# Other orders of instructions around a recurrence's front, its inverse and a gate, and two squares on ScalarE

## The reference

```python
# first block
z = rms_norm(x, attn_norm) @ w_in            # 1024 pool columns, then r, k, v and three small ones
zs = token_shift(z[..., 1024:], mu_shift)    # zf + (z_prev - zf) * mu
...
def step(S, inp):                            # per head of 64, over the tokens
    r_t, w_t, k_t, v_t, a_t, b_t = inp
    sa = einsum('bhij,bhj->bhi', S, a_t)
    S = S * w_t + sa[..., None] * b_t + v_t[..., None] * k_t
    y = einsum('bhij,bhj->bhi', S, r_t)
...
x = x + concatenate([pool_out, rwkv_out]) @ w_out
x = x + square(relu(rms_norm(x) @ w_ffn_up)) @ w_ffn_down
x = x + sigmoid(rms_norm(x, ple_norm) @ w_ple_gate) * (p @ w_ple_proj)
x = rms_norm(x, final_norm)
# second block: gated linear attention and a sparse attention side by side
proj = rms_norm_2(x, attn_norm_g) @ w_in_2
h = x + concatenate([gla_mixer(...), nsa_mixer(...)]) @ w_out_2
out = h + (silu(m @ w_gate) * (m @ w_up)) @ w_down    # m = rms_norm_2(h, ffn_norm_g)
```

## Time and profile before

| | us |
|---|---|
| median of 3 runs | 2287.65 |
| their lowest and highest | 2287.09, 2288.55 |
| the profiled execution | 2290.27 |
| its span, first to last instruction | 2288.5 |
| PE busy | 2266.2 (99%) |
| DVE busy | 1458.3 (64%) |
| ACT busy | 978.5 (43%) |
| POOL busy | 177.8 (8%) |

### The profile page before, as it was taken

How to read it: one execution, slowest core, us unless ns; L and a number is a source line. 1 busy time by engine, 2 the same in 40 slices (tenths; PEclk the granted TensorE clock), 3 DMA queues, 4 the chain that set the end, 5 groups by cost and what they waited for, 6 DMA issues and landing times.

```text
span 2288.5 us, 34500 instructions
## 1 busy us (share of the span) xinstructions
PE 2266.2 (99%) x15676; PEld 2057.7 (90%) x15676; DVE 1458.3 (64%) x1214; ACT 978.5 (43%) x929; POOL 177.8 (8%) x138
## 2 busy tenths in 40 slices
PE   9999999999999999999999999999999999999999
PEld 8998988998998988988889999888998998999898
DVE  6699676665664665565558559786665665565564
ACT  5653245433333333344544364475343433433432
POOL 1004110010110110110000001100000000001000
PEclk9999999999999999999999999999999999999999
DMA  8553166656656656666556655345555655665644
GB/s 252 173 164 88 33 222 207 200 205 199 205 200 204 199 206 197 208 223 209 176 178 195 186 187 148 111 151 184 185 197 197 225 190 184 221 209 178 226 161 147
DMA packets 335306, 425.06 MB, mean 186 GB/s; under 512 B 4521, under 2 KB 249625, under 8 KB 334777
## 3 DMA queue, kind: packets, MB, share of 16 engines
q1 hardware_dynamic: 333465, 418.50, 56.3%
q0 software_dynamic: 1552, 4.23, 0.6%
q10 hardware_dynamic: 144, 0.13, 0.0%
HBM read 420.75 MB, written 2.10 MB: 185 GB/s over the span
## 4 chain that ended last, share of the span: by engine, by line
PE 92%; DVE 6%; ACT 1%; issue 0%; DMA 0%; DVEq 0%; SPq 0%; ACTq 0%
PE PS L673 50%; PE PS L719 23%; PE PS L721 11%; PE PS L937 1%; DVE ring_r L2197 1%; PE PS L718 1%; PE PS L738 1%; PE PS L1129 1%; DVE ring_r L2532 1%; PE PS L856 0%; ACT arena_r L1527 0%; PE PS L1010 0%; PE PS L1065 0%; PE PS L1057 0%; PE PS L1319 0%
## 5 line engine op out<-in xcount | busy, mean ns | idle before, releaser
L1527 ACT ACTIVATE arena_r<-ring 128x2048 fp32r<-128x2048 f32 (+1 forms) x394 | 690.1, 1760 | 940.7 <-PE PS L673 542.3
L2139 DVE TENSOR_TENSOR ring_r<-ring,arena_r 128x2048 fp32r<-128x2048 f32 x316 | 721.6, 2290 | 489.7 <-ACT arena_r L1527 489.7
L719 PE MATMUL PS<-arena_r,arena_r 128*128 128x512 f32 x2432 | 789.7, 382 | 0.0
L673 PE MATMUL PS<-arena_r,arena_r 128*128 128x512 f32 (+2 forms) x2128 | 707.5, 346 | 1.7 <-DVE ring_r L2532 0.9
L721 PE MATMUL PS<-arena_r,ring_r 128*128 128x256 f32 x2280 | 621.5, 273 | 0.0
L673 PE MATMUL PS<-ring_r,arena_r 128*128 128x512 f32 (+1 forms) x1504 | 523.3, 361 | 1.2 <-DVE ring_r L2197 1.2
L719 PEld LDWEIGHTS PS<-arena_r,arena_r 128*128 128x128 f32 x2432 | 449.1, 189 | 56.3
L673 PE MATMUL PS<-arena_r,actT_r 128*128 128x512 f32 (+1 forms) x1184 | 442.1, 373 | 0.0
L673 PEld LDWEIGHTS PS<-arena_r,arena_r 128*128 128x128 f32 (+1 forms) x2128 | 401.5, 189 | 44.1 <-issue 4.8
L721 PEld LDWEIGHTS PS<-arena_r,ring_r 128*128 128x128 f32 x2280 | 437.4, 192 | 3.9
L673 PEld LDWEIGHTS PS<-ring_r,arena_r 128*128 128x128 f32 x1504 | 277.5, 190 | 35.7 <-issue 3.1
(11 more groups left out here) (381 smaller groups left out, 1648.5 us busy)
## 6 DMA issues: line engine op xcount, KB each, us to landing
ring<-in_w_ffn_up SPq DMA_DIRECT2D x32, 2048.0 KB, 9.6
ring<-in_w_ffn_down SPq DMA_DIRECT2D x32, 2048.0 KB, 7.9
ring<-in_w_in SPq DMA_DIRECT2D x22, 2048.0 KB, 8.3
ring<-in_w_gate SPq DMA_DIRECT2D x22, 2048.0 KB, 8.1
ring<-in_w_up SPq DMA_DIRECT2D x22, 2048.0 KB, 8.2
ring<-in_w_in SPq DMA_DIRECT2D x32, 1024.0 KB, 5.2
ring<-in_w_out SPq DMA_DIRECT2D x16, 2048.0 KB, 9.1
ring<-in_w_down SPq DMA_DIRECT2D x12, 2048.0 KB, 8.1
```

Source lines behind the costliest of these rows:

```text
L673: mm = pe.matmul(dst, r32(w, early)[rows], r32(x, early)[rows], start=first and q == 0, stop=last and q == 2)
L719: mm = pe.matmul(dst, r32(wh[:, k, c]), r32(beside(high, low)), start=x == 0, stop=x == KT - 1)
L1527: return act.activation(dst, src, ACT.Copy, scale=scale)
L2139: v.tensor_tensor(r32(u), u, high_of(high_home(n, i, j)), ALU.subtract).then_inc(S["w_low"], counts(units, j))
```

## The change

On DVE the AR block goes behind `low1(6, 0)`, the low parts of unit 6 move forward by one place each, and only one of them is left between the BK products. In the inverse PE does `pool_tile(4, 0, range(4))` ahead of corners A and `range(4, 8)` between the two `turn_v`; DVE does the first two `block_turned` of the last level behind its `block_added`, and the memsets ahead of the last corner copies, with a new wait. Behind the gates `low(N_GLA, (2,))` and `low(N_GLA, (3,))` go to later places on DVE, and ACT makes the tokens' high parts before their squares. In the attention the two squares go from POOL to ACT, between high halves, with the waits that they had.

```diff
--- before.py
+++ after.py
@@ -975,14 +975,15 @@
                 inverse_group(g, 4 + g % 2, lambda h, m, c, e: DTi[h, m, c, :], lambda h, m, c, e: Fi[h, m, c, :])\
                     .then_inc(S["df_ready"], 1)
 
+        pool_tile(2 + (len(LEVELS) - 1) // 2, 0, range(4))
         for g in range(2):
             pe.wait_ge(S["d_added"], 4 * (len(LEVELS) - 2) + 2 * g + 2)
             corner_group(g, INV[g], LATE, lambda m, c, e: G[EARLIER[e], m, e, c, B32:C],
                          lambda m, c, e: Di[EARLIER[e], m, c, 0:B32]).then_inc(S["f_ready"], 1)
         pe.wait_ge(S["shifted"], 3)
-        for c in range(2):
-            turn_v(c)
-        pool_half(len(LEVELS) - 1)
+        turn_v(0)
+        pool_tile(2 + (len(LEVELS) - 1) // 2, 0, range(4, 8))
+        turn_v(1)
         for g in range(2):
             pe.wait_ge(S["dt_turned"], 4 * (len(LEVELS) - 2) + 2 * g + 2)
             pe.wait_ge(S["f_masked"], 4 * (len(LEVELS) - 1) + 2 * g + 2)
@@ -1826,7 +1827,8 @@
             n = N_GLA + c
             high(n, (3,))
             if c == 0:
-                norm_chunk("n4", None, 3)
+                tokens_high("n4", None, 3)
+                squares("n4", 3)
                 for q in range(4):
                     scaled_squares(q)
                 root("n4")
@@ -1885,7 +1887,15 @@
         high_half(g1, 7)
         high_half(g2, 0, 1)
         level_exps(4, 5)
-        high_half(g2, 2, 3, 4, 5, 6, 7)
+        high_half(g2, 2, 3)
+        act.wait_ge(S["gqk_ready"], 1)
+        act.wait_ge(S["level_ready"], len(GLA_HALF))
+        act.wait_ge(S["groups_read"], 11)
+        act.activation(KSQ, NK[:, 4:8, :], ACT.Square).then_inc(S["nsq_ready"], 1)
+        high_half(g2, 4)
+        act.wait_ge(S["groups_read"], 13)
+        act.activation(QSQ, GOQ[:, 8:16, :], ACT.Square).then_inc(S["nsq_ready"], 1)
+        high_half(g2, 5, 6, 7)
         high_half(g3, 0, 1)
         act.wait_ge(S["k_var"], 1)
         act.activation(RK, RK, ACT.Sqrt).then_inc(S["k_root"], 1)
@@ -2253,12 +2263,6 @@
         link(reciprocals(6, 2))
         link(v.tensor_tensor(kk, kk, tmp1, ALU.mult))
 
-        v.wait_ge(S["head_acts"], 3)
-        lwc, kkc = (a.rearrange("p m (c j) -> p (m c) j", c=NCH) for a in (lw, kk))
-        arf = AR.rearrange("p m c j -> p (m c) j")
-        v.tensor_copy(PEND.rearrange("p m c -> p (m c)"), lwc[:, :, C - 1])
-        v.tensor_scalar(arf[:, :, 0:1], kkc[:, :, 0:1], -1.0, None, ALU.mult)
-        v.scalar_tensor_tensor(arf[:, :, 1:C], lwc[:, :, 0:C - 1], -1.0, kkc[:, :, 1:C], ALU.mult, ALU.mult)
         low1(5, 2)
         v.wait_ge(S["z_copied"], 6)
         link(shift(0, VM))
@@ -2273,19 +2277,27 @@
             ins = v.scalar_tensor_tensor(tmp1[:, m, :], zr[:, m, :], col("r_k", m), zk[:, m, :], ALU.mult, ALU.mult)
         ins.then_inc(S["rkr_ready"], 1)
         low1(6, 0)
+
+        def chunks(a):
+            return a.rearrange("p m (c j) -> p m c j", c=NCH)
+
+        v.wait_ge(S["head_acts"], 3)
+        lwc, kkc = (a.rearrange("p m (c j) -> p (m c) j", c=NCH) for a in (lw, kk))
+        arf = AR.rearrange("p m c j -> p (m c) j")
+        v.tensor_copy(PEND.rearrange("p m c -> p (m c)"), lwc[:, :, C - 1])
+        v.tensor_scalar(arf[:, :, 0:1], kkc[:, :, 0:1], -1.0, None, ALU.mult)
+        v.scalar_tensor_tensor(arf[:, :, 1:C], lwc[:, :, 0:C - 1], -1.0, kkc[:, :, 1:C], ALU.mult, ALU.mult)
+        low1(6, 1)
         v.tensor_tensor(ga, kk, ga, ALU.mult)
         v.wait_ge(S["rkr_ready"], 1)
-
-        def chunks(a):
-            return a.rearrange("p m (c j) -> p m c j", c=NCH)
-
         v.tensor_tensor(AR[:, :, :, C:P], chunks(zr), chunks(lw), ALU.mult).then_inc(S["ar_ready"], 1)
-        low1(6, 1)
+        low1(6, 2)
         v.wait_ge(S["ar_ready"], 1)
         for e in range(2):
             h = HALF[e]
             v.tensor_tensor(BK[h, :, :, e * C:(e + 1) * C], chunks(ga)[h], chunks(tmp2)[h], ALU.mult)
-            low1(6, 2 + e)
+            if e == 0:
+                low1(6, 3)
             ins = v.tensor_tensor(BK[h, :, :, (1 - e) * C:(2 - e) * C], chunks(zk)[h], chunks(tmp2)[h], ALU.mult)
         ins.then_inc(S["bk_ready"], 1)
         v.wait_ge(S["z_copied"], 7)
@@ -2377,26 +2389,29 @@
                 mask_copied(LO, slice(0, C))
             block_added(lv, 0)
             block_added(lv, 1)
-            block_turned(lv, 0)
+            if lv < len(LEVELS) - 2:
+                block_turned(lv, 0)
             block_added(lv, 2)
-            block_turned(lv, 1)
+            if lv < len(LEVELS) - 2:
+                block_turned(lv, 1)
             block_added(lv, 3)
-            block_turned(lv, 2)
-            block_turned(lv, 3)
+            for g in range(2 if lv < len(LEVELS) - 2 else 0, 4):
+                block_turned(lv, g)
         for g in range(2):
             v.wait_ge(S["f_ready"], 4 * (len(LEVELS) - 1) + g + 1)
             for e in range(2):
                 v.tensor_copy(corners(Fi, g, LATE[e], slice(0, B32)), bank16(INV[g], LATE[e])).then_inc(S["f_masked"], 1)
         low1(8, 1)
+        v.wait_ge(S["dt_turned"], 4 * (len(LEVELS) - 1))
+        v.memset(SD[0], 0.0)
+        for e in range(2):
+            v.memset(UV(0)[HALF[e], :, e, :], 0.0).then_inc(S[f"s_placed{e}"], 1)
         for g in range(2):
             v.wait_ge(S["corner_ready"], g + 1)
             for e in range(2):
                 v.tensor_copy(corners(DTi, g, EARLIER[e], slice(B32, C)), bank16(INV[2 + g], EARLIER[e]))\
                     .then_inc(S["corner_placed"], 1)
 
-        v.memset(SD[0], 0.0)
-        for e in range(2):
-            v.memset(UV(0)[HALF[e], :, e, :], 0.0).then_inc(S[f"s_placed{e}"], 1)
         gsq = area(8 * ZW, 16, C)
 
         def group_squares(t):
@@ -2518,7 +2533,7 @@
                 rms("n3", rs_gate).then_inc(S["rs_ready"], 1)
             else:
                 tokens_low("n4", None, c - 1)
-            low(n + 1, (0, 1, 2))
+            low(n + 1, (0, 1, 2) if c < 3 else (0, 1))
             v.wait_ge(S["groups_read"], c + 1)
             v.wait_ge(S["proj_ready"], c + 1)
             link(v.tensor_tensor(gate_sb, PS[:, 4:6, :], gate_sb, ALU.mult))
@@ -2556,12 +2571,15 @@
 
         for c in range(4):
             n = N_GLA + c
-            low(n, (3,))
+            if c:
+                low(n, (3,))
             if c == 0:
                 tokens_low("n4", None, 3)
+                low(n, (2,))
                 for q in range(4):
                     scale_residual(q)
                 link(rms("n4", rs_fin))
+                low(n, (3,))
                 v.wait_ge(S["chunk_summed"], SUMMED["scaled"])
                 link(v.tensor_reduce(scaled_ss, scaled_sums, AX, ALU.add))
                 for _ in range(2):
@@ -3046,12 +3064,6 @@
         pool.wait_ge(S["side_loaded"], SIDE + 48)
         pool.dma_start(glamask.rearrange("p n j -> p (n j)"), consts[:, GLAMASK_AT:]).then_inc(S["side_loaded"], 16)
 
-        pool.wait_ge(S["gqk_ready"], 1)
-        pool.wait_ge(S["level_ready"], len(GLA_HALF))
-        pool.wait_ge(S["groups_read"], 11)
-        pool.tensor_tensor(KSQ, NK[:, 4:8, :], NK[:, 4:8, :], ALU.mult).then_inc(S["nsq_ready"], 1)
-        pool.wait_ge(S["groups_read"], 13)
-        pool.tensor_tensor(QSQ, GOQ[:, 8:16, :], GOQ[:, 8:16, :], ALU.mult).then_inc(S["nsq_ready"], 1)
         pool.wait_ge(S["gsc_summed"], len(GLA_HALF))
         for i, n in enumerate(("k", "v")):
             pool.dma_start(PTAB[i], W[f"cmp_{n}_pos_2"]).then_inc(S["side_loaded"], 16)
```

## The result

The changed kernel takes 2292.03 us (median of 12 runs, 2290.65 to 2293.36), the kernel before in the same comparison 2287.55 us (12 runs, 2286.43 to 2290.34): 4.5 us more, ratio 1.0020 with a 95% interval of 1.0012 to 1.0027. The forecast was 2288.5 in a range of 2283.0 to 2293.0, so the time lies inside, 3.5 us above the point; it is nearer to the times of the rivals E (2293.0) and B (2293.3) than to the forecast's own. The profiled execution took 2293.1 us (span 2291.3), 2.8 more than the profiled one of before.

What follows compares the result with a forecast made beforehand. TensorE is busy 2266.2 of 2288.5 us, so only its waits, instructions and clock count. Front +1.9, inverse −4.5, gates +4.4 and attention −1.0 sum to +0.8 us: 2288.5 us, range 2283.0 to 2293.0.

Steps and rivals of the forecast that it cites:

- Rival E: Inverse: the new order brings nothing, as DVE's copies bind the last level; sum +5.3, 2293.0 us; chance 0.06.
- rival B: Clock stays 0.50 for 6.8 us behind the gates and still falls in the inverse; +5.6, 2293.3 us; chance 0.10.
- front: BK transposes: fifth group waits for a first copy queued behind a shift and low part 7,0; +1.9 us.
- inverse: Inverse up to L1020: full products among small ones hold the clock, memsets go earlier; −4.5 us, other bound −2.3.
- gates, order: Behind the gates: turn and tokens sooner (−1.7), but unit 3's low part behind the norm's root makes PE late; +3.1 us.
- gates, clock: Behind the gates: after 4.8 us of idle PE the clock falls for a while; 0 to 3.4 us, +1.3 taken.
- attention: Attention: squares on ACT free DVE's low halves from GpSimd, so PE's 0.86 us wait and slower start go; −1.0 us.
- Rival A: Gates: PE is not held by the last low part, −1.7 for +4.4; sum −5.3, 2282.4 us; chance 0.15.

Runs made afterwards that it cites:

- the swap: Changed gates' order alone, with the low part of unit 3 ahead of the final norm's rms instead of behind: 2287.58 against 2287.52 us for the kernel before.

## Why the prediction was right, and where it was off

The profiles' column is by the starts of the same products in the profiles of the kernel before and of the changed one.

| term | forecast | two profiles | alone, by medians |
|---|---|---|---|
| front | +1.9 | +1.9 (0.3 gained ahead of the heads is in it) | +2.3 |
| inverse | −4.5 | −4.7 | −1.75 |
| gates, order | +3.1 | +3.1 | |
| gates, clock | +1.3 | +2.9 | together +5.7 |
| attention | −1.0 | −1.1 | −1.0 |
| scores: clock | not foreseen | +1.6 | |
| gaps without a reason in the inverse's earlier products; before 72 us | not foreseen | −1.0; +0.1 | |
| sum | +0.8 | +2.8 | +4.5 (all in one) |

**What bounds it** held in the main: PE's waits and its clock account for the difference, but for 1.0 us of gaps that no wait explains and that differ between profiles of one order. The reading of PE's waits was incomplete: the second largest, 2.3 us of the scores (L898) for DVE's masks, is none of the places that the change touches, and it is unchanged after it.

**Front**: each number came, the copy at 177.93 (177.92), the fifth group at 178.67 (178.66). The move of `low1(7, 0)` behind the copies shows the cause.

**Inverse**: the 4.7 us of the two profiles match the 4.5 forecast, but more than half of that is luck. The wait for the memsets went, as the prediction had it (1.0 us), and so did the gap in the corners (0.7 to 1.0 us, of which it counted on 0.5). The rest was to come from the clock, and there the step that failed is the base. The sum took the earlier trace rows as the kernel before and put the fall of the clock down to its order, small products without full ones among them. But seven profiles of the same order keep 1.00 there, so that order alone does not make the clock fall. The 2.3 to 2.8 us that the fall costs (17.95 less 15.68 or 15.13) are in the profiled 2290.27 us and not in the median of 2287.65. The prediction saw that difference of 2.6 us and carried it over as if it were the same for both kernels. Had it been read as the fall, the inverse would have been worth 1.9 and the time 2291 us. That is 2.6 of the 3.6 us by which the difference to before was missed (+4.5 for +0.9). Rival E, by which the inverse brings nothing, fell too.

**Gates, order**: all steps came, the turn 1.05 us sooner, tokens 1.7 us sooner (from the same products), unit 3 at +3.1. Rival A fell; its remaining question, whether the wait could be had away, was answered by moving one line, and then the next low part was late, which A had not counted.

**Gates, clock**: forecast between 0 and 3.4 with 1.3 taken, measured 2.9 to 3.0: the whole length of 6.8 us at 0.50, half of what rival B names. Its other half (the fall in the inverse stays) did not come. With idle of 4.6 us the choice of a middle value had no row behind it; the row that was nearest, a fall of 6.8 us after far less idle, was the one to take. That is another 1.6 us. With −0.1 for the attention these make 4.1 us where 3.6 were missed. The difference of 0.5 us, in which the fall in the scores lies too, is within the interval of the ratio (2 us).

**Attention**: −1.0 came. The table load that the Trainium skill ("ScalarE activation tables: per-element evaluation and per-set limits", section "What a function is on this engine") states between functions of two sets, 1283 ns, did not come for Square after copies: ACT's row in the changed kernel has none there.

**The range** was 10 us wide. The time lay in it although two terms were 2.6 and 1.6 us off in the same direction, so that it was right says little for the sum.

Still open: what decides in which executions the clock falls in the scores or in the inverse. It differs from run to run with the same kernel, and no experiment here was made to steer it. That the late low part makes the clock fall is shown by the swap. That each execution of the changed kernel has that fall is only likely: none of its twelve runs has a mean clock of 1.000, but the three with 0.999 leave room for one fall only, which may be this one or that in the scores.

## What to carry to other kernels

Before a sum is made on a profiled execution, ask whether its clock falls are of every run: compare its time and mean clock with those of the runs, and where it stands 2.6 us above the median, look for what in its trace is worth 2.6 us. When a step is moved behind a norm, find the longest chain of another engine that the norm waits for, as the step is as late as that chain; and after a wait is gone, work out which low part is late next before the gain is booked.

## What the runs showed of the hardware

TensorE's clock fell to 0.50 (1.2 of 2.4 GHz) for 6.8 us in both profiles with 4.6 us of idle PE, 0.7 to 0.9 us before the idle ended. For 3.4 or 6.8 us it also fell in the scores or in the inverse, stretches of small products with short waits, and there only in some executions: one of eight profiles of the old order in the inverse, three of all fourteen in the scores. A fall of 6.8 us was worth 2.3 to 3.0 us, as much as one of the edits; a fall of 3.4 us was worth 1.6 us in two profiles and nothing in the third, where waits of PE went in exchange.

VectorE's subtraction that began beside GpSimd's square of 4.51 us took 4.6 us; in the kernels with the square on ScalarE it took 1.2 us. Of these 3.4 us only what PE had waited for was gained, 0.86 us at one low half (1.1 us by the starts of products).
